# The split weights of a three-product float32 kernel moved to 32 modulo 128

## The reference, cut to what matters

```python
h = rms_norm(x, attn_norm[l]); proj = h @ w_in[l]
...
x = x + (jax.nn.silu(h @ w_ffn_gate[l]) * (h @ w_ffn_up[l])) @ w_ffn_down[l]
```

## Time and profile before

| | |
|---|---|
| median of 3 runs (lowest, highest) | 1059.9 us (1058.3, 1060.31) |
| span of the profiled execution | 1057.7 us |
| mean granted TensorE clock | 1.000 |
| matmuls / loads of weights | 8,760 / 8,760 |
| HBM read | 184.98 MB, 176 GB/s |

### The profile page before, as it was taken

How to read it: one execution, slowest core, us unless ns; L and a number is a source line. 1 busy time by engine, 2 the same in 40 slices (tenths; PEclk the granted TensorE clock), 3 DMA queues, 4 the chain that set the end, 5 groups by cost and what they waited for, 6 DMA issues and landing times.

```text
span 1057.7 us, 22212 instructions
## 1 busy us (share of the span) xinstructions
PE 1047.9 (99%) x8760; PEld 1020.3 (96%) x8760; DVE 741.0 (70%) x1098; ACT 579.6 (55%) x880; POOL 77.0 (7%) x92
## 2 busy tenths in 40 slices
PE   9999999999999999999999999999999999999998
PEld 8899999999999999999999999898889999999998
DVE  6799988747876666657666677667986876665666
ACT  5456655576565544556544445455666664554553
POOL 0000000001310000111000001041001300000110
PEclk9999999999999999999999999999999999999999
DMA  6356433344556554555555456464335455554563
GB/s 235 129 173 217 162 123 120 120 160 170 190 181 217 190 186 146 198 204 190 205 196 194 148 193 217 173 207 162 137 120 199 171 191 196 198 203 146 195 222 120
DMA packets 32444, 187.81 MB, mean 178 GB/s; under 512 B 3832, under 2 KB 7552, under 8 KB 14720
## 3 DMA queue, kind: packets, MB, share of 16 engines
q1 hardware_dynamic: 31472, 185.58, 50.3%
q0 software_dynamic: 416, 1.06, 0.4%
q10 hardware_dynamic: 496, 0.33, 0.2%
HBM read 184.98 MB, written 1.06 MB: 176 GB/s over the span
## 4 chain that ended last, share of the span: by engine, by line
PE 87%; DVE 6%; ACT 1%; issue 1%; DVEq 0%; ACTq 0%
PE acc L681 83%; PE area_a L681 2%; PE area_t L681 2%; DVE wlo L1575 2%; DVE s_sum L2133 0%; ACT he L1179 0%; ACT whi L1179 0%; PE area_t L947 0%; ACT s_a L1179 0%; DVE mask L1780 0%; DVE st L1765 0%; DVE score L1805 0%; DVE s_z L2135 0%; DVE s_a L2131 0%; DVE s_z L2037 0%
## 5 line engine op out<-in xcount | busy, mean ns | idle before, releaser
L681 PE MATMUL acc<-hs,whi 128*128 128x256 f32 x3584 | 624.6, 279 | 2.9 <-DVE wlo L1575 2.7
L681 PEld LDWEIGHTS acc<-hs,whi 128*128 128x128 f32 x3584 | 541.9, 187 | 10.1 <-issue 7.1
L681 PE MATMUL acc<-hs,wlo 128*128 128x256 f32 x1792 | 496.8, 277 | 0.0
L1179 ACT ACTIVATE whi<-raw 128x1024 fp32r<-128x1024 f32 (+3 forms) x379 | 357.2, 978 | 162.8 <-PE acc L681 136.6
L1575 DVE TENSOR_TENSOR wlo<-raw,whi 128x1024 fp32r<-128x1024 f32 (+4 forms) x259 | 272.1, 1092 | 98.5 <-ACT whi L1179 97.4
L681 PEld LDWEIGHTS acc<-hs,wlo 128*128 128x128 f32 x1792 | 336.1, 188 | 0.2
L681 PE MATMUL acc<-hid,whi 128*128 128x256 f32 x1056 | 180.9, 277 | 0.2 <-DVE wlo L1575 0.2
L681 PEld LDWEIGHTS acc<-hid,whi 128*128 128x128 f32 x1056 | 159.2, 188 | 0.4 <-DVE wlo L1575 0.4
L681 PE MATMUL acc<-hid,wlo 128*128 128x256 f32 x528 | 146.0, 277 | 0.0
L1663 DVE TENSOR_TENSOR wlo<-raw,whi 128x1024 fp32r<-128x1024 f32 x120 | 141.2, 1219 | 4.3 <-ACT whi L1179 4.2
L1676 DVE TENSOR_TENSOR hbuf<-acc,sbuf 128x256 f32<-128x256 f32 x66 | 28.0, 425 | 115.4 <-PE acc L681 112.0
(11 more groups left out here) (316 smaller groups left out, 1029.2 us busy)
## 6 DMA issues: line engine op xcount, KB each, us to landing
raw<-in_w_gu SPq DMA_DIRECT2D x66, 1024.0 KB, 4.8
raw<-in_w_dn SPq DMA_DIRECT2D x48, 704.0 KB, 4.0
raw<-in_w_up SPq DMA_DIRECT2D x10, 1024.0 KB, 4.8
raw<-in_w_gates1b SPq DMA_DIRECT2D x8, 1024.0 KB, 4.7
raw<-in_w_out SPq DMA_DIRECT2D x8, 1024.0 KB, 4.8
raw<-in_w_qk SPq DMA_DIRECT2D x8, 1024.0 KB, 4.8
raw<-in_w_gates SPq DMA_DIRECT2D x8, 1024.0 KB, 4.8
raw<-in_w_projT_b SPq DMA_DIRECT2D x7, 1024.0 KB, 4.8
```

The costliest lines, as they stand in the source:

```text
L681: return nc.tensor.matmul(out, w, m, start=start, stop=stop, skip_group_check=True)
L1179: return nc.scalar.activation(out, in_, f, **kw)
```

## The change

`whi` and `wlo` begin 32 bytes later, at 41,376 and 58,016. Everything allocated behind `wlo` begins 32 + 96 = 128 bytes later and so keeps its place modulo 128; `x` and `raw` stay. No instruction is added, removed or moved.

```diff
         x = fixed("x", (KD, T))
         raw = fixed("raw", (2, SLOT))
+        top[0] += 32
         whi = fixed("whi", (2, SLOT), F32R)
         wlo = fixed("wlo", (2, SLOT), F32R)
+        top[0] += 96
         tmp = fixed("tmp", (4, T))
         con = fixed("con", (N_CONST,))
```

## The result

| | before | after |
|---|---|---|
| median of 4 runs (lowest, highest) | 1059.5 us (1058.3, 1060.31) | 1079.26 us (1079.14, 1079.36) |
| span of the profiled execution | 1057.7 us | 1077.3 us |

The ratio is 1.0186, with a 95% interval of 1.0171 to 1.020: 19.8 us slower, where no change was forecast and 1075 was the end of the range. The kernel before has one run more here than in the table ahead of the prediction.

A forecast was written before the change was run, and what follows sets the result against it. TensorE was taken as the bound: number of matmuls times the distance between starts. Four terms of 0 left the profiled 1057.7 us unchanged; with 2.2 us up to the runs' median the forecast was 1060 us, range 1050 to 1075.

The forecast's parts named there:

- Term (1): Loading weights from 32 modulo 128, some 7,900 times: taken as 0 us, with bounds of +25 and -23 us.
- the long spacing: 117.8 ns between matmul starts, about 2,170 of 7,787 spacings in 128x256 blocks; the other 5,620 are short, 113.3 ns.
- Rows 8: Trace rows of weight loads: those of `ones`, from 32 modulo 128, take 188 ns, as `whi` does.
- Rows 8 and 9: Load durations, and back-to-back load pairs from 32 and from 64, both 0.30 us; read as showing no address effect.
- rival C: Long spacing spreads in loops `gu` and `dn`: 1084.9 us if all short blocks turn, 1072 if half; chance 0.27.
- Rows 11: Forget logits' 8-column weights, from 0 and 32 in turn: three matmuls take 0.34 us in one place, 0.35 in the other.
- Term (2): `whi` and `wlo` as moving operand in token-major products, going from 0 to 32: taken as 0, within 0.5 us.
- Term (3): ScalarE writing `whi`, VectorE reading it and writing `wlo`, at 32: taken as 0, at most +0.4 us.
- Term (4): Everything behind `wlo` moves 128 bytes, place modulo 128 kept: taken as 0 us.
- B: Rival: the long matmul spacing falls away, 1050.3 us, partly so 1050 to 1057; chance 0.18, below 113.3 ns 0.03.
- A: The forecast case: the address is not seen anywhere, 1058 to 1062 us; chance 0.52.
- The page's 109.2 ns: Skill page's matmul distance, N/2.4 + 2.5 ns for 256 columns; by it the kernel would be an estimated 42 us faster.

The follow-up runs named there:

- D = 0: Moving operand's start less weights' start, modulo 128, is 0: weights moved to 64, the moving operands' place, against the kernel before; 1093.09 us.
- D = 64: Moving operand starts 64 bytes behind the weights modulo 128, as in the kernel before (weights 0, moving operands 64); 1059.5 us.
- D = 32: Moving operand starts 32 bytes behind the weights modulo 128: the changed kernel, weights at 32 instead of the kernel before's 0; 1079.26 us.
- D = 96: Moving operand starts 96 bytes behind the weights modulo 128: against the kernel before, weights stay at 0, everything behind wlo 32 bytes later; 1092.25 us.
- D = 56: Moving operand starts 56 bytes behind the weights modulo 128: weights 8 bytes later than in the kernel before, moving operands at 64; 1084.1 us.

## Why the prediction was wrong, point by point

**What bounds the kernel: right.** The time is the number of matmuls times their distance; no wait came or went, and the 256-column distances hold all of the 19.6 us (20.4, with 0.8 given back elsewhere).

**Term (1), the load from 32: the step that failed.** I took 0, and it was +20.4 us. That it lies inside the bound of +25 is luck: the bound took the long spacing for the worst that an address can do, and at D = 0 the blocks that were short have 119.3 ns and those that were long 119.1, 33.6 us in all. Three rows were read for more than they could say.
- *Rows 8* give the duration of the load. It is 188 ns at D = 64 and at D = 32, and 190 at D = 0. It was no witness.
- *Rows 8 and 9* show loads from 32 (`con`) beside float32 products. Their moving stream runs at half the rate (215 ns from start to start for 256 columns), and I had noted so myself under rival C, but did not take it off the value of the evidence. Beside a full-rate stream there was the earlier trace rows alone, in a long block, and long blocks are just those that lose nothing (117.7 and 117.7).
- *Rows 11* show full-rate streams beside loads from 0 and 32 in turn, with the short spacing in one place. I wrote that the start at 32 was already among these rows. The start was, but not a load of 128 columns: with 16 columns a bad distance costs 0.2 ns, with 128 it costs 3.5. That the spacing does not fall with short loads (true in the main: 1054 us and 113.5 ns with 16 columns) does not mean that it cannot rise with long ones. It is a limit that can be passed from one side.

Behind all three lies one error of framing. I asked whether the trace has a load *from 32*, and all kernels with D = 64 answer that this is harmless (1059.42 us with everything moved by 32). The question was whether the trace has a full-rate stream of 256 columns and a full load at *another distance than 64*. In the chains of weights there is not one, as every moving operand lies at 64 and `whi` and `wlo` at 0. But a few single loads from `con` have D = 32 beside such a stream, and the earlier trace rows shows only one in a long block, where the distance is long anyway. The same load comes again at 710.40 us at the end of a short block (timeline of PE, kernel before):

```profile
710.40 0.28 PE L681 MATMUL acc<-hs,wlo 128*128 128x256 f32 x1
710.52 0.59 PE L681 MATMUL area_t<-n2sq,con 128*128 128x512 f32 x1
```

The distance there is 116 ns behind steady ones of 113 and 114; at 88.50 and 225.96 us, where blocks with the short spacing also end in a load from `con`, it is 117 and 116. This is no proof: where a chain gives way to other operands, single distances vary at D = 64 too (113 before `zhi` at 28.38 us, 119 behind it, 115 before `he` at 208.62). Yet these were the nearest rows, they showed 2 to 4 ns where there was room for 1.6, and the prediction does not weigh them. Its 0 rested on rows that were further off.

**Term (2), token-major products: nearly right.** Of the 204 distances 48 have 136 columns and keep their mean of 112.9 ns; the others went from 231.6 to 232.9, which is the 0.2 us counted above, within the 0.5. The products of `fvl`, three in four of which have another distance than 64 by their row pitch, were a sign for 512 columns only: those went up by 1.3 ns with this change, those of 256 columns in the `gu0` loop by 3.7.

**Term (3), ScalarE and VectorE: right, and it was 0.** With everything at 32 the time is that of before. In the changed kernel the halves of the subtraction have nearly the length of before (groups of VectorE by form, mean ns; before 1219 and 1230). The 1243 is not the address: with the weights at 0 and D = 96 it is 1244.

```profile
L1665 DVE TENSOR_TENSOR wlo<-raw,whi 128x1024 fp32r<-128x1024 f32 x120 | 141.1, 1218 | 3.7 <-ACT whi L1181 3.7
...
L1577 DVE TENSOR_TENSOR wlo<-raw,whi 128x1024 fp32r<-128x1024 f32 x155 | 186.2, 1243 | 52.8 <-ACT whi L1181 51.9 <-DVE h L1979 0.2
```

**Term (4), the 128 bytes: right**, 1059.33 us.

**The rivals.** C gave the direction, the place (the `gu` and `dn` loops) and nearly the size: 1084.9 if all short blocks became long, and they went to 117.3 instead of 117.8, less steadily. Part of that nearness is luck, as other distances pass C's ceiling of 1084.9 by 7 to 10 us. Its condition, that the load beside a full-rate stream needs more room than the short spacing leaves, agrees with the pairs with short loads but is not shown. Its wording, a load *from 32*, is refuted: D = 64 from 32 is free. The range left out the upper part of C, at 0.12, and the time lies there. B did not happen at any address tried: no changed kernel with full loads came under 1059.3 us. A was the likeliest case by rows that could not tell it from C.

**The page's 109.2 ns.** In the section that the prediction cites for it ("Back-to-back issue gap" of the Trainium skill's page "TensorE: Matmul & The Clock Gate") this is the distance of isolated matmuls; of a stream of loads and matmuls the section says that both set the spacing. The estimate of 42 us was therefore not for a chain like this one.

**What stays open.** Why 64 of seven distances is the good one, and why one load of three at D = 32 costs more than three, was not settled; I know the price by address, not what meets what inside. Nor is it settled what chooses between 113.3 and 117.8 at equal addresses. That mix is still worth 9.6 us by the prediction's estimate, and shorter loads shift it: with 16-column loads the blocks that were long have 114.3 ns. No version of the full computation tried here beats the kernel before.

## What to carry to other kernels

Where a float32r matmul streams 256 columns and a full load of weights runs beside it, try first the moving operand 64 bytes behind the weights modulo 128, all weights of a chain alike, and keep it so when anything ahead of them in SBUF changes size: on this kernel, the only one measured, it is worth 20 to 35 us of 1060 against the other distances tried. An address is to be judged by its distance to the other operand in flight, not by itself. A row is evidence for an edit only if it has the same stream rate and the same length of load; equal durations of single loads are none, so compare the distances of starts.

## What the runs showed of the hardware that was not expected

- With full loads beside full-rate matmuls the pace depends on the difference of the two start addresses: 113.3 ns from start to start in `gu0` at D = 64, 117.0 at D = 32, 119.1 to 119.3 at D = 0, 80 and 96, with 256 columns and a granted clock of 1.00 throughout.
- A shift of the weights by 8 bytes is enough: D = 56 costs 24.7 us more than D = 64.
- In multiples of 32 bytes it does not matter where the pair lies as a whole: 0 and 64, 32 and 96 give 1059.5 and 1059.4 us; 0 and 96, 96 and 64 give 1092.25 and 1092.2.
- Prices do not add: `wlo` alone at D = 32 costs 35 us, `whi` and `wlo` together 20.
- At D = 64 loads of 16 columns bring a little: 1053.95 us against 1059.9 beside it. The 1058.2 us with 64 columns lies within the spread of the kernel before, though the blocks that were long go from 117.8 to 116.7 ns in its trace.
